# The Fox layer's norm: inverse root multiplied in when key, query, value and gate chunks are evicted

## The reference, cut to what matters

```python
def rmsnorm(x, g):
    y = x * lax.rsqrt(jnp.mean(x * x, axis=-1, keepdims=True) + RMS_EPS)
    return y * g
...
x = x + jnp.square(relu(rmsnorm(x, norm_ff_g[0]) @ ff_w1[0])) @ ff_w2[0]
hk = rmsnorm(x, kv_norm_g)
kvf = hk @ kvf_w                      # k: 1024, v: 1024, forget gate: 16 columns
log_f = log_sigmoid(kvf[..., 2 * D:] + fgate_b)
c_bhs = cumsum(log_f, axis=1)
h = rmsnorm(x, norm_mix_g[1])
q = h @ fox_wq
s = q k^T / 8 + (c_q - c_k), causal; p = softmax(s); x = x + (p v) @ fox_wo
```

## Time and profile before

| | |
|---|---|
| median of three runs | 1542.17 us (1541.81 to 1542.85) |
| profiled execution, its own time | 1540.85 us |
| its span | 1539.1 us |
| TensorE busy | 1473.5 us, 96% of the span |
| VectorE busy | 1094.2 us, 71% |
| ScalarE busy | 684.7 us, 44% |
| mean granted TensorE clock | 0.982 of full speed |

### The profile page before, as it was taken

The page is one execution under the profiler, slowest core; times in us unless marked ns, Lnnn a source line. Parts: engine busy times, 40 slices in busy tenths (PEclk is TensorE's granted clock), DMA queues, the critical chain, the costliest instruction groups (busy, mean ns, idle before and its releaser), DMA issues.

```text
span 1539.1 us, 21324 instructions
## 1 busy us (share of the span) xinstructions
PE 1473.5 (96%) x8244; PEld 1268.4 (82%) x8244; DVE 1094.2 (71%) x1636; ACT 684.7 (44%) x884; POOL 30.3 (2%) x20
## 2 busy tenths in 40 slices
PE   7999998999999999989999979998999988999997
PEld 6878887888887777878888868887788876888886
DVE  3799366788777775658887669987646748777653
ACT  2322344555334443545543355553444346465542
POOL 0000000000000000000000000000003400000000
PEclk9999999999999999999999999999999998999999
DMA  8544533355775544525557827757644324455451
GB/s 316 197 152 169 159 129 110 119 209 204 273 251 185 190 167 148 174 76 189 191 208 275 280 98 278 276 192 259 228 164 155 106 75 156 159 172 186 146 177 58
DMA packets 60190, 279.27 MB, mean 181 GB/s; under 512 B 6633, under 2 KB 8106, under 8 KB 35275
## 3 DMA queue, kind: packets, MB, share of 16 engines
q1 hardware_dynamic: 55672, 266.49, 49.8%
q10 hardware_dynamic: 4434, 11.64, 2.1%
HBM read 273.89 MB, written 4.19 MB: 181 GB/s over the span
## 4 chain that ended last, share of the span: by engine, by line
PE 84%; DVE 9%; DMA 4%; ACT 3%; issue 1%; DVEq 0%; ACTq 0%; SPq 0%
PE acc L433 40%; PE acc L435 20%; PE acc L454 10%; DMA ada_w<-in_ada 3%; PE stat L600 3%; PE acc L542 2%; DVE wsplit L1451 2%; PE stat L702 1%; PE score L664 1%; PE acc L546 1%; DVE ada_w L1739 1%; DVE tsum L1603 1%; PE score L872 1%; PE acc L485 1%; PE turned L684 1%
## 5 line engine op out<-in xcount | busy, mean ns | idle before, releaser
L433 PE MATMUL acc<-hA,wsplit 128*128 128x512 f32 x1728 | 615.6, 401 | 8.8 <-DVE hA L1591 6.7
L435 PE MATMUL acc<-hA,wsplit 128*128 128x256 f32 x1728 | 484.8, 281 | 0.0
L982 ACT ACTIVATE wsplit<-raw 128x2048 fp32r<-128x2048 f32 (+2 forms) x206 | 366.0, 1777 | 209.1 <-PE acc L435 204.0
L1451 DVE TENSOR_TENSOR wsplit<-raw,wsplit 128x2048 fp32r<-128x2048 f32 (+2 forms) x206 | 436.3, 2120 | 9.2 <-ACT wsplit L982 9.2
L433 PEld LDWEIGHTS acc<-hA,wsplit 128*128 128x128 f32 x1728 | 327.1, 189 | 89.8 <-issue 11.8
L435 PEld LDWEIGHTS acc<-hA,wsplit 128*128 128x128 f32 x1728 | 328.5, 190 | 0.3
L433 PE MATMUL acc<-hid,wsplit 128*128 128x512 f32 x864 | 303.8, 394 | 0.0
L435 PE MATMUL acc<-hid,wsplit 128*128 128x256 f32 x864 | 244.0, 282 | 0.0
L433 PEld LDWEIGHTS acc<-hid,wsplit 128*128 128x128 f32 x864 | 162.8, 188 | 34.3
L992 ACT ACTIVATE lowp<-acc 128x512 f32<-128x512 f32 x126 | 73.9, 587 | 243.6 <-PE acc L435 216.2
L435 PEld LDWEIGHTS acc<-hid,wsplit 128*128 128x128 f32 x864 | 163.8, 190 | 0.4
(11 more groups left out here) (233 smaller groups left out, 1742.5 us busy)
## 6 DMA issues: line engine op xcount, KB each, us to landing
raw<-in_gu SPq DMA_DIRECT2D x44, 1024.0 KB, 4.9
ada_w<-in_ada SPq DMA_DIRECT2D x144, 256.0 KB, 4.7
raw<-in_up SPq DMA_DIRECT2D x32, 1024.0 KB, 4.9
raw<-in_down SPq DMA_DIRECT2D x32, 1024.0 KB, 5.0
raw<-in_dn SPq DMA_DIRECT2D x32, 704.0 KB, 4.1
raw<-in_pw SPq DMA_DIRECT2D x8, 1024.0 KB, 6.5
raw<-in_memk SPq DMA_DIRECT2D x8, 1024.0 KB, 5.0
raw<-in_memv SPq DMA_DIRECT2D x8, 1024.0 KB, 5.3
```

Source lines behind the costliest of these rows:

```text
L433: nc.tensor.matmul(dst.rearrange("p (s t) -> p s t", s=2), w, h, start=start, stop=False, skip_group_check=True)
L435: return nc.tensor.matmul(dst[:, 0:T], lo_w, h[:, 0, :], start=False, stop=stop, skip_group_check=True)
L982: nc.scalar.activation(wsplit[:, slot, 0, 0:elems_of(n)], raw[:, slot, 0:elems_of(n)], ACT.Copy).then_inc(S("w_hi"), 1)
L1451: V.tensor_tensor(wsplit[:, slot, 1, 0:e], src, wsplit[:, slot, 0, 0:e].bitcast(F32), ALU.subtract).then_inc(S("w_lo"), 1)
```

## The change

"fox" joins the deferred norms. The operands hA and hB hold x times the weights alone. hA's pairs are made during down0, hB's behind its last sum, around `norm_scale`. The q and k chunks, whose results have the rows of x along the free axis, are multiplied by `rstd` with one further VectorE instruction. The v and gate chunks have the rows on the partitions. For them TensorE transposes `rstd`, VectorE copies one column of each half to `rcol`, and both the eviction by ScalarE and the sum by VectorE multiply by that column, a row tile at a time. k0 starts in parts as hA's pairs come ready, with the last sum of squares inside. The filler matmuls behind down0 are gone, since the stage no longer waits for the norm. One ADA tile moves from down0's last chunk to gu1.

```diff
-DEFERRED = {"memq0": "memq0", "up0": "ff0", "memq1": "memq1", "up1": "ff1"}
+DEFERRED = {"memq0": "memq0", "up0": "ff0", **{f"fox{s}{g}": "fox" for g in range(4) for s in "kq"},
+            "memq1": "memq1", "up1": "ff1"}
+
+ROW_SCALED = ["foxf", "foxv0", "foxv1", "foxv2", "foxv3"]
...
-ADA_STAGES = [("down0", 16), *[... fox ...], ("down1", 16), ("gu1", 16), ("dn1", 12)]
+ADA_STAGES = [("down0", 15), *[... fox ...], ("down1", 16), ("gu1", 17), ("dn1", 12)]
...
 # TensorE
                 def begin():
+                    if st.chunks == 1:
+                        for p in range(PAIRS):
+                            if p == PAIRS - 1:
+                                norm_sums(DEFERRED[name], [PAIRS - 1])
+                            part(0, p)
+                        return
...
-            fox_chunk("k0")(0, 0)
+                begin, chunk = linear(f"fox{name}", hB if name[0] == "q" else hA, ready, steps=True)
+                return begin if name == "k0" else chunk
+
+            fox_chunk("k0")()
             linear("foxf", hA, None)
+            pe.wait_ge(S("norm_rstd"), 3 * (norm_index("fox") + 1))
+            for tt in range(TT):
+                mm = nc.tensor.transpose(turned[:, tt, 0:P], rstd[:, tt * P:(tt + 1) * P], ident[:])
+            mm.then_inc(S("rcol_turn"), 1)
             fox_chunk("v0")(0, 0)
...
 # ScalarE
+                if st.name in ROW_SCALED:
+
+                    wait("rcol", 1)
+                    for tt in range(TT):
+                        last = nc.scalar.activation(lowp[:, tt, 0:width], acc[:, par, tt, width:2 * width], ACT.Copy,
+                                                    scale=rcol[:, tt:tt + 1])
...
                 def flush():
                     log_table(norm_name)
                     pair_done(PAIRS - 1)
+                    if norm_name == "fox":
+                        norm_hi("fox", dests[1], 1, pairs=[0, 1])
...
                 norm_root(norm_name)
+                if norm_name == "fox":
+                    norm_hi("fox", dests[1], 1, pairs=[2, 3])
...
 # VectorE
+                if st.name in ROW_SCALED:
+                    for tt in range(TT):
+                        last = V.scalar_tensor_tensor(out=dst[:, tt, :], in0=acc[:, par, tt, 0:width],
+                                                      scalar=rcol[:, tt:tt + 1], in1=lowp[:, tt, 0:width],
+                                                      op0=ALU.mult, op1=ALU.add)
+                    last.then_inc(S("acc_summed"), 1)
+                    return
...
+                def other(p, low):
+                    if low:
+                        operand_lo(second[0], p, second[1], 1)
+                    else:
+                        operand_h(second[0], p, x, second[2], 1)
...
+                def before(c, known):
+                    if not operand or known < st.per_acc:
+                        return
+                    if known % st.per_acc == (1 if st.per_acc > 1 else 0):
+                        operand_lo(operand[0], known // st.per_acc - 1 if st.per_acc > 1 else c - 1, operand[1])
...
+                def urgent():
+                    other(0, False)
+                    last_operand()
+
+                linear(name, combine=combine, before=before, urgent=urgent)
+                other(1, False)
+                other(0, True)
+                other(2, False)
+                other(1, True)
+                norm_scale(operand[0])
+                other(3, False)
+                other(2, True)
+                other(3, True)
...
-            feed_forward("up0", "down0")
-
-
-            norm("fox", x, [(hA, lambda kt: col("kv", kt)), (hB, lambda kt: col("mix1", kt))])
+            feed_forward("up0", "down0", operand=("fox", hA, lambda kt: col("kv", kt)),
+                         second=("fox", hB, lambda kt: col("mix1", kt)))
...
             fox_chunk("k0")
+            wait("rcol_turn", 1)
+            V.tensor_copy(rcol[:], turned[:, :, 0]).then_inc(S("rcol"), 1)
             linear("foxf", dest=lambda a: small[:, 0, :].rearrange("p (r n) -> p r n", r=TT), width=HEADS)
```

More of the change, by code:

```diff
@@ L146 @@
               ("moba", G_HEADS, G_HEADS)]
-ADA_STAGES = [("down0", 16), *[(f"fox{s}{g}", 1) for g, order in enumerate(["kvq"] + 3 * ["kqv"]) for s in order], ("down1", 16), ("gu1", 16), ("dn1", 12)]
+ADA_STAGES = [("down0", 15), *[(f"fox{s}{g}", 1) for g, order in enumerate(["kvq"] + 3 * ["kqv"]) for s in order], ("down1", 16), ("gu1", 17), ("dn1", 12)]
 ADA_SLOTS = [(name, c) for name, n in ADA_STAGES for c in range(n)]
@@ L220, in program @@
         var = place("var", [P, T])
+        rcol = place("rcol", [P, TT])
         cols = place("cols", [P, NCOL])
@@ L783, in fox_chunk @@
                 ready = pair_ready(nb) if name == "k0" else pair_ready(nb + PAIRS) if name == "q0" else None
-                return linear(f"fox{name}", hB if name[0] == "q" else hA, ready, steps=True)[1]
-            fox_chunk("k0")(0, 0)
+                begin, chunk = linear(f"fox{name}", hB if name[0] == "q" else hA, ready, steps=True)
+                return begin if name == "k0" else chunk
+            fox_chunk("k0")()
             linear("foxf", hA, None)
+            pe.wait_ge(S("norm_rstd"), 3 * (norm_index("fox") + 1))
+            for tt in range(TT):
+                mm = nc.tensor.transpose(turned[:, tt, 0:P], rstd[:, tt * P:(tt + 1) * P], ident[:])
+            mm.then_inc(S("rcol_turn"), 1)
             fox_chunk("v0")(0, 0)
@@ L991, in low @@
                     wait("acc_summed", a + st.acc_base)
-                last = nc.scalar.activation(lowp[:, :, 0:width], acc[:, par, :, width:2 * width], ACT.Copy)
+                if st.name in ROW_SCALED:
[4 more added lines that the diff above has]
+                else:
+                    last = nc.scalar.activation(lowp[:, :, 0:width], acc[:, par, :, width:2 * width], ACT.Copy)
                 last.then_inc(S("acc_low"), 1)
@@ L1464, in total @@
                     return
+                if st.name in ROW_SCALED:
[5 more added lines that the diff above has]
+                    return
                 V.tensor_tensor(dst, acc[:, par, :, 0:width], lowp[:, :, 0:width], ALU.add).then_inc(S("acc_summed"), 1)
             def linear(name, dest=None, before=None, early=None, post=None, flush=None, width=T, straight=False,
-                       steps=False, combine=None):
+                       steps=False, combine=None, urgent=None):
                 st = STAGE[name]
@@ L1479, in body @@
                         combine(a, ka)
+                        if urgent and known == st.chunks - 1:
+                            urgent()
                     elif last:
                         if known == 0 and name in DEFERRED:
-                            wait("norm_lo", norm_base(DEFERRED[name]) + PAIRS)
+                            q = norm_index(DEFERRED[name])
+                            wait("norm_lo", norm_base(DEFERRED[name]) + PAIRS * NORMS[q][1])
                         if dest is None or name in DEFERRED:
@@ L1506, in linear, with operand_h @@
                     flush()
-            def operand_h(norm_name, p, src, gain):
-                if p >= 2:
-                    wait("norm_lo", norm_base(norm_name) + p - 1)
+            def operand_h(norm_name, p, src, gain, which=0):
+                if PAIRS * which + p >= 2:
+                    wait("norm_lo", norm_base(norm_name) + PAIRS * which + p - 1)
                 for j in range(2):
@@ L1516, in operand_h, with operand_lo, add_to_x @@
                 last.then_inc(S("norm_h"), 1)
-            def operand_lo(norm_name, p, dest):
-                wait("norm_hi", norm_base(norm_name) + p + 1)
+            def operand_lo(norm_name, p, dest, which=0):
+                wait("norm_hi", norm_base(norm_name) + PAIRS * which + p + 1)
                 V.tensor_tensor(dest[:, 2 * p:2 * p + 2, T:2 * T], tsum[:, p % 2, :, :],
                                 dest[:, 2 * p:2 * p + 2, 0:T].bitcast(F32), ALU.subtract).then_inc(S("norm_lo"), 1)
-            def add_to_x(name, gain=None, bias=None, operand=None):
+            def add_to_x(name, gain=None, bias=None, operand=None, second=None):
                 st = STAGE[name]
@@ L1552, in combine, with last_operand @@
                         operand_h(operand[0], a, x, operand[2])
[L1554 to L1558, removed]
+                def other(p, low):
+                    if low:
+                        operand_lo(second[0], p, second[1], 1)
+                    else:
+                        operand_h(second[0], p, x, second[2], 1)
[4 more added lines that the diff above has]
+                        operand_lo(operand[0], known // st.per_acc - 1 if st.per_acc > 1 else c - 1, operand[1])
+                def last_operand():
+                    if operand:
+                        operand_lo(operand[0], PAIRS - 1, operand[1])
+                if not second:
+                    linear(name, combine=combine, before=before, flush=last_operand)
```

(13 more changed lines are left out.)

## The result

The changed kernel takes 1547.79 us (median of 6 runs, 1544.89 to 1552.12). The kernel before, timed beside it, took 1540.76 (6 runs, 1535.71 to 1542.85). The ratio is 1.0050, 95% interval [1.0034, 1.0066]. So the change costs 0.5%, where 1541.7 and "within 0.2%" were forecast. The profiled execution took 1544.89 us around a span of 1543.1, the fastest of the six; its mean granted clock is 0.982, as before.

The account below looks back on a forecast made before the run. TensorE was taken to bound the kernel (84% of the chain), VectorE the stretch between down0 and Fox. A gain of 4.3 us less 3.8 lost in the heads took 1542.17 to 1541.7 us, range 1537.8 to 1545.0.

Parts of the forecast that it names:

- within 0.2%: Whole kernel: no change beyond 0.2% (3.1 us), about what a measurement tells from no change; chance 0.70.
- What bounds the kernel; down0's cover: TensorE holds 84% of the chain; in down0 it is always busy, so VectorE's added work there has cover.
- The start of Fox: From down0's end to the first scores: VectorE's shorter queue brings the first scores 4.3 us earlier.
- The heads: Fox heads: VectorE's extra work delays heads 2 (1.3 us), 6 (0.9) and 10 to 12 (1.6), 3.8 lost.
- The first rival: Heads: VectorE catches up, only 0.35 us is lost, gain 3.95 us, 1538.2 us; chance 0.20.
- Other parts, "nothing": Outside Fox: hA pairs made in down0 and the ADA tile moved to gu1 are covered and cost nothing.
- its sum, 4.3 - 3.8: Whole kernel: gain at Fox's start less loss in the heads, 0.5 us earlier, 1541.7 us.
- the clock falls again: Rival, v0 and heads 2, 6, 10, 12: TensorE's waits lower the clock, 2.9 us per fall, two give 1547.6; chance 0.10.
- gu1 covers the tile: gu1: the moved ADA tile costs nothing because VectorE has room and TensorE never stops; 1.6 us if uncovered.

Follow-up runs that it names:

- e3: The kernel before plus one further VectorE instruction (0.72 us) for each of k1, q1, k2, q2, k3, q3: 1545.83 us, ratio to the kernel before 1.0033.
- e1: The changed kernel with the ADA tiles of q1, q2 and q3 moved to gu1: 1544.62 us, ratio to the kernel before 1.0022.
- e5: The changed kernel with rcol placed behind all other SBUF tiles, only addresses differing: 1543.54 us, ratio to the kernel before 1.0020.
- e6: The kernel before with an unused 32-byte tile between var and cols: 1547.51 us, ratio to the kernel before 1.0040.
- e7: The kernel before with an unused 64-byte tile between var and cols: 1545.02 us, ratio to the kernel before 1.0033.
- e9: The kernel before with an unused 32-byte tile behind ada_w, so only the large region moves: 1545.17 us, ratio to the kernel before 1.0024.
- e2: The changed kernel with 12, 7, 7 and 20 filler matmuls ahead of TensorE's waits at turns 2, 6, 10 and 12: 1544.40 us, ratio 1.0019.
- e11: The changed kernel with rcol at the end, ADA tiles of q1, q2, q3 in gu1, and 18 filler matmuls ahead of turn 12: 1537.53 us, ratio 0.9978.
- e8: The changed kernel with rcol at the end and the ADA tiles of q1, q2 and q3 in gu1: 1537.34 us, ratio to the kernel before 0.9978.
- e4: The changed kernel without the multiplication by the root for k1 to k3 and q1 to q3 (not usable): 1543.89 us, ratio to the kernel before 1.0014.

## Why the prediction was wrong

**What bounds the kernel; down0's cover.** Right. TensorE never stopped in down0, and its moved products cost nothing there.

**The start of Fox.** Right in its order and nearly in its size. VectorE's low half of hA stood at 478.16, 4.03 us behind x's sum where 4.5 was read from memo0. k0's sum came at 487.23, 13.1 us behind x's; 13.7 was worked out. v0 started at 488.79, with the idle time of 2.90 that the removed fillers leave, and again with a half clock: 0.66 from 482 to 497, a stretch of 10.2 us at 1.2 GHz (483.4 to 493.6), of which 4.8 lie in v0. The running sum at 496.83 and the scores at 507.98 give a gain of 4.86 for the 4.3 predicted. The scores still waited for the three transfers, as forecast: the row names fq, but that instruction started at 506.30 and took 0.69 us, and the last transfer was issued at 504.1 and takes 3.9 us to land (the median of the three). VectorE's two row-scaled instructions of v0 took 0.88 us, as estimated; ScalarE's two took 0.84 for the 0.6 of one whole activation, where 0.1 more was assumed.

**The heads.** Right. 1.56, 0.88, 0.86 and 0.72 more at turns 2, 6, 10 and 12 stand against 1.3, 0.9 and, for heads 10 to 12, 1.6. e3 shows that this is the second pass, with the same waits and the same 3.7 us in the kernel before. The first rival, that the heads absorb it, falls. The waits hang on the ADA tiles behind q1, q2 and q3 as well: without them (e1) VectorE absorbs all but head 12's.

**Other parts, "nothing".** This step failed. The prediction costed every instruction and none of the addresses: its sum, 4.3 - 3.8, has no term for a slower TensorE in stages whose instructions did not change. The new tile `rcol` moves hid and its neighbours by 32 bytes, and TensorE's pairs on them go from 346.7 ns to between 349 and 353. Measured: the changed kernel takes 4.3 us more than the one with rcol elsewhere (e5), its own profile shows 4.5 us in the pairs on the region, and moving the region in the kernel before costs 3.7 to 6.2 us (0.0024 to 0.0040 of 1541 us; e6, e7, e9). The 4.3 alone take 1541.7 past the end of the range at 1545.0. From the kernel before as timed beside it, 1540.8 in place of 1542.2, they reach 1544.6, and the clock below has a part in the miss.

**The clock.** The rival "the clock falls again" was right that falls would come, and its price and its number of falls were off. A new stretch in the heads lasts 3.4 us and costs 1.7, not 2.9; two came, one behind turn 6 and one behind the first scores. The second cannot be put down to the new waits: it lies ahead of them all, and e7 and e9 have it without the change. e2 gives 3.4 us back by filling the waits. e3 has nearly the same waits and no such stretch, and e11's fillers gave nothing back, so this term is not a fixed price per wait, and its size over a whole execution stays open: from 0.9 us (the two profiles) to 3.4 (e2).

**gu1 covers the tile.** Right: behind the wait at its start (5.7 us, as before) TensorE waited once in gu1, for 0.2 us, and the three tiles more of e8 did not stop it from being the fastest.

**Sum.** From 1540.8 (before, beside it): -4.8 for the start, +4.0 for the heads, +3.4 for the clock and +4.3 for rcol's place give 1547.7, and 1547.79 was measured. The agreement to 0.1 is luck. The first three terms are from one execution, the fastest of the six, the last is a difference of medians that is uncertain by about 3 us, and with the clock's 0.9 of the whole span the sum is 1545.2. The start's gain is read from the profiles alone; that the waits in the heads and rcol's place are real is shown by runs of their own (e3, e5). A change with both losses mended is 0.2% faster than the kernel before (e8), so the sign of the result hung on these two.

What stays open: why 32 bytes matter. 32 and 64 bytes both slow the pair, and with 32 its level changes within a stage and from one execution to the next. 96 and 128 bytes were not tried. The stages that read hA, which has not moved, have a second cause. gu2 lies on either level in kernels of either kind: 353.3 ns in the profile before, 346.7 in that after. up0 and up1 took 346.7 or 346.8 ns in all seven profiles in which `cols` to `ada_w` lay in their old place or 64 bytes on, and in the changed kernel; in e1, e2, e4 and e6, where these small tiles are 32 bytes further, 353.2 in seven stages of eight. At 6.5 ns for 512 pairs that is 3.3 us, which could be why e6 lost more than e9; no run moves the small tiles alone. The profile of the changed kernel shows none of it, and its own time is 2.9 us below the median.

## What to carry to other kernels

A new small tile is an edit of every address behind it. Place it behind the large operands, or time the kernel before with an unused tile of that size, before the change itself is judged. When work is moved from a stretch that is bound by VectorE to evictions spread over later chunks, look for what else stands ahead of the tight places and can move (here three ADA tiles): the change lost 0.5% as it was, and gains 0.2% with the tile placed last and those tiles moved. Turn every new wait of TensorE into a question about the clock, but price it as a chance, and count the granted clock over the whole span before a stretch is charged to the change. Take a pace from a whole stage: seven pairs gave 353 ns where the stage's mean was 350.

## What the runs showed of the hardware

- The pace of identical fp32r matmul pairs at a granted clock of 1.00 depends on where the moving operand lies in SBUF: in the stages on hid 346.7 to 346.8 ns in its old place, 350.0 to 350.1 with it 64 bytes further (e7), 348.9 to 353.4 with 32 (six profiles).
- A wait of TensorE of 0.88 us among large matmuls was followed by 3.4 us at 1.2 GHz in one profile (turn 6, 562.0 in the changed kernel), one of 0.75 by none in another (e3). At turn 12 a wait of 1.84 us was followed by 6.8 us at 1.2 GHz in the kernel before, one of 1.82 by none in e9.
- With 18 to 20 small filler matmuls in the wait at turn 12, 2.4 GHz was granted behind it (e2, e11). The median came down by 3.4 us in one case and not at all in the other.
